# First norm with tokens on the partitions and transposes on TensorE, x loaded a second time; out projection, second norm and first FFN blocks interleaved by tile; last third of the FFN by tile

## What is computed

```python
mod = (jax.nn.silu(c) @ w_ada[l] + b_ada[l])[:, None, :]
sh1, sc1, ga1, sh2, sc2, ga2 = jnp.split(mod, N_MOD, axis=-1)
h = rms_norm(x, g_mix[l]) * (1 + sc1) + sh1
z = h @ w_in[l] + b_in[l]          # q k v | conv B, C, x | two gates; 50 blocks of 128 columns
attn = sliding_window_sink_attention(q, k, v, sinks[l])      # window 128, 16 heads of 64
conv = conv_b * causal_depthwise_conv(conv_c * conv_x, conv_w[l])
merged = jax.nn.sigmoid(gate_a) * attn + jax.nn.sigmoid(gate_c) * conv
x = x + ga1 * (merged @ w_out[l])
h = rms_norm(x, g_ffn[l]) * (1 + sc2) + sh2
gu = h @ w_ffn_in[l]
g_part, u_part = jnp.split(gu, 2, axis=-1)                   # 2816 each
x = x + ga2 * ((jax.nn.silu(g_part) * u_part) @ w_ffn_out[l])
return rms_norm(x, g_final)
```

## Time and profile before

| | us |
|---|---|
| three runs, median (lowest, highest) | 1123.89 (1123.4, 1236.33) |
| the profiled execution | 1121.86 |
| its span, core 5 | 1120.3 |
| spans of all cores | 1116.9 to 1120.3 |
| TensorE busy | 973.4 |
| VectorE busy | 634.0 |
| ScalarE busy | 350.8 |
| GpSimd busy | 250.6 |

### The profile page before, as it was taken

How to read it: one execution, slowest core, us unless ns; L and a number is a source line. 1 busy time by engine, 2 the same in 40 slices (tenths; PEclk the granted TensorE clock), 3 DMA queues, 4 the chain that set the end, 5 groups by cost and what they waited for, 6 DMA issues and landing times.

```text
span 1120.3 us, 15109 instructions; the slowest of 8 cores (1116.9 to 1120.3 us)
## 1 busy us (share of the span) xinstructions
PE 973.4 (87%) x5445; PEld 446.8 (40%) x5445; DVE 634.0 (57%) x834; ACT 350.8 (31%) x525; POOL 250.6 (22%) x276
## 2 busy tenths in 40 slices
PE   0273629999999999999979999999999999999972
PEld 0141214444444444444434434444444444444441
DVE  3449575595877969696977651134222243112697
ACT  3144124555454545454334321100111100111331
POOL 3405342121202111121365610000100001000460
PEclk9997669999999999999999999999999999999985
DMA  9950215886303031221610433210522205200124
GB/s 214 199 144 0 38 28 86 121 114 73 47 11 57 10 49 29 29 39 20 95 19 1 75 48 48 38 20 1 85 38 38 38 1 73 40 10 1 51 101 150
DMA packets 42201, 63.84 MB, mean 57 GB/s; under 512 B 19200, under 2 KB 21376, under 8 KB 40080
## 3 DMA queue, kind: packets, MB, share of 16 engines
q0 software_dynamic: 20304, 45.36, 26.6%
q1 hardware_dynamic: 21824, 17.52, 5.4%
HBM read 99.76 MB, written 8.45 MB: 97 GB/s over the span
## 4 chain that ended last, share of the span: by engine, by line
PE 79%; DVE 8%; issue 6%; ACT 3%; DMA 3%; POOL 1%; SPq 0%; DVEq 0%; ACTq 0%; POOLq 0%
PE psum L524 32%; PE psum L880 25%; PE psum L893 12%; PE psum L836 4%; PE psum L677 3%; DVE h L467 3%; DMA xres<-xt 3%; DVE xres L911 2%; PE psum L653 2%; POOL sqB L479 1%; DVE rs L455 1%; ACT L453 1%; PE psum L450 1%; DVE h L460 0%; DVE rden L702 0%
## 5 line engine op out<-in xcount | busy, mean ns | idle before, releaser
L524 PE MATMUL psum<-h,ws 128*128 128x512 bf16 (+2 forms) x1744 | 374.3, 368 | 23.1 <-DVE h L467 23.1
L880 PE MATMUL psum<-h,fws 128*128 128x512 bf16 x1408 | 305.7, 379 | 6.3 <-DVE h L467 4.9
L524 PEld LDWEIGHTS psum<-h,ws 128*128 128x128 bf16 x1744 | 163.0, 99 | 201.8 <-issue 51.0
L880 PEld LDWEIGHTS psum<-h,fws 128*128 128x128 bf16 x1408 | 137.3, 98 | 174.2 <-issue 9.7
L888 DVE TENSOR_TENSOR mg<-psum,sg 128x512 bf16<-128x512 f32 x88 | 60.6, 691 | 221.2 <-PE psum L880 216.4
L893 PE MATMUL psum<-mg,fwo 128*128 128x512 bf16 (+1 forms) x760 | 157.3, 370 | 11.5 <-DVE xres L900 9.9
L885 ACT ACTIVATE sg<-psum 128x512 bf16<-128x512 f32 x88 | 52.5, 597 | 336.3 <-PE psum L880 331.1
L702 DVE RECIPROCAL rden<-rden 128x256 f32<-128x256 f32 x64 | 110.5, 1737 | 7.7 <-ACT rden L700 7.2
L893 PEld LDWEIGHTS psum<-mg,fwo 128*128 128x128 bf16 x760 | 75.5, 100 | 94.4 <-issue 15.5
L900 DVE SCALAR_TENSOR_TENSOR xres<-psum,modc,xres 128x512 f32<-128x512 f32 (+1 forms) x104 | 72.0, 704 | 66.1 <-PE psum L893 66.1
L828 POOL TENSOR_TENSOR acc<-acc,sq 128x512 f32<-128x512 f32 (+1 forms) x56 | 79.6, 1426 | 116.1 <-ACT sq L826 111.8
(11 more groups left out here) (95 smaller groups left out, 716.1 us busy)
## 6 DMA issues: line engine op xcount, KB each, us to landing
ws<-w_in_l POOLq DMA_DIRECT2D x50, 256.0 KB, 4.7
fws<-w_fi_l POOLq DMA_DIRECT2D x44, 256.0 KB, 4.8
xres<-xt SPq DMA_DIRECT2D x8, 1024.0 KB, 18.4
wadaB<-w_ada_l POOLq DMA_DIRECT2D x8, 1024.0 KB, 10.1
out<-xres SPq DMA_DIRECT2D x12, 512.0 KB, 3.2
fwo<-w_fo_l POOLq DMA_DIRECT2D x22, 256.0 KB, 6.4
wadaA<-w_ada_l POOLq DMA_DIRECT2D x4, 512.0 KB, 24.0
wadaB<-w_ada_l POOLq DMA_DIRECT2D x4, 512.0 KB, 37.1
```

Source lines behind the costliest of these rows:

```text
L524: P.op("pe", [lambda e, k=k: e.matmul(bank(b)[:, 0:n], lhsT=WS[s * 1024 + k * 128, s * 1024 + (k + 1) * 128], rhs=hk(k, col, n), start=(k ...
L880: P.op("pe", [lambda e, k=k, s=s, b=b: e.matmul(bank(b), lhsT=FS[s * 1024 + k * 128, s * 1024 + (k + 1) * 128], rhs=hk(k, 128 + tt * 512, ...
```

## The change

First norm. x is loaded with tokens on the partitions (`xtok`, new input, same bytes). `stats` squares 1024 channels of 128 tokens at a time on ScalarE with the sum as a by-product, `roots` takes root and reciprocal of one value per token, `scale` multiplies by that (into `xn`, bf16), and `turn` transposes the 8 x 4 blocks of a tile on TensorE, 8 to a PSUM bank, and reads them out of PSUM with scale and shift applied, into `h`. The sums on GpSimd and VectorE, the fp32 matmuls, the reciprocal of 512 columns, `scaled` and `affine` are gone for the first norm. `prep` of tile t + 1 stands ahead of tile t's projections and `turned` behind them. The halo's k and v are made behind tile 0's projections.

Loads. x tile 1 waits for the second quarter of `wadaB`, the weights of slots 4 to 7 and the mask for x tile 1, x tile 2 for tile 1 and tile 3 for tile 2. In step c = 3 all of x is loaded again, in the old layout, 8 MB.

Second norm. `scaled` becomes 8 instructions of 512 columns at a later priority. Out projection, second norm and the first three FFN blocks are written in the order w0 w1 w2 f0 w3 f1 f2 f3, and all 8 banks are in rotation from w0 on. In the last third of the FFN, whose 14 weight blocks are now all loaded ahead, each tile runs `ff_in`, `ff_out` and the final norm before the next tile starts.

The planner. For every engine but TensorE it now takes, of the ready operations that could start within 0.25 us of the first, the one of lowest priority number. Operations of the same role are at L522 (`turn`), L556 (`mods_cols`), L584 (`group`), L607 (v transposes), L712 and L736 (attention), L900 (`w_out`), L468 (fp32 matmul), L953 (`ff_in`) and L966 (`ff_out`) of the new file.

```diff
--- before.py
+++ after.py
...
+    WINDOW = 0.25
...
-            best = None
+            first = None
             for e in self.ENGS:
                 f = free[e]
                 for o in ready[e]:
-                    k = (max(f, o.start), o.prio, o.idx)
+                    k = max(f, o.start)
+                    if first is None or k < first[0]:
+                        first = (k, e)
+            e = first[1]
+            lim = first[0] + (0.0 if e == "pe" else self.WINDOW)
+            best = None
+            for o in ready[e]:
+                at = max(free[e], o.start)
+                if at <= lim:
+                    k = (o.prio, o.idx)
                     if best is None or k < best[0]:
-                        best = (k, o)
+                        best = (k, o, at)
...
+    XN0 = buf("xn0", A_AT + 12320, 4096, BF16)
+    XNH = buf("xnH", A_AT + 20512, 1024, BF16)
+    XN = buf("xn", A_MG + 4096, 4096, BF16)
...
+    F2 = buf("fws2", A_K, 4096, BF16)
+    F3 = buf("fws3", A_AT + 34848, 2048, BF16)
...
-        P.op("sp", lambda e: e.dma_start(out=XH.t[:], in_=xhalo_d), writes=[XH.iv()], dma="d_xh", cost=0.1, nbytes=524288)
...
-        load_x(0)
-        load_x(1)
+        load_x(0, xtok_d)
+        P.op("sp", lambda e: e.dma_start(out=XH.t[:], in_=xhalo_d), writes=[XH.iv()], dma="d_xh", cost=0.1, nbytes=524288)
...
-        load_x(2, after=(last_wa,))
+        x1 = load_x(1, xtok_d, after=(wa_parts[1],))
         for zi in range(4, 8):
-            load_z(zi)
-        load_x(3, after=(last_wa,))
+            load_z(zi, after=(x1,))
...
+        x2 = load_x(2, xtok_d, after=(x1,))
+        load_x(3, xtok_d, after=(x2,))
...
+        def stats(src, a, nblk, s0, out):
+            for i in range(nblk):
+                P.op("act", lambda e, i=i: e.activation(out=out[i * 1024, (i + 1) * 1024], in_=src[a + i * 1024, a + (i + 1) * 1024],
+                                                        func=AF.Square, accum_out=SS[s0 + i, s0 + i + 1]),
...
+        def roots(s0, n):
+            P.op("act", lambda e: e.activation(out=RSTD[s0, s0 + n], in_=SS[s0, s0 + n], func=AF.Sqrt, bias=EPSC.t[:], scale=1.0 / D),
...
+            P.op("dve", lambda e: e.reciprocal(out=RSTD[s0, s0 + n], in_=RSTD[s0, s0 + n]),
...
+        def turn(xn, nblk, hcol, bks, engs):
...
+                P.op("pe", [lambda e, j=j, i=i, g=g, tp=tp: e.transpose(tp[:, j * n + i * 128:j * n + (i + 1) * 128],
+                                                                 xn[i * 1024 + (g * per + j) * 128, i * 1024 + (g * per + j + 1) * 128],
+                                                                 IDENT.t[:]) for j in range(per) for i in range(nblk)],
...
+                        P.op("dve", lambda e, k=k, src=src: e.tensor_scalar(out=hk(k, hcol, n), in0=src, scalar1=A1[k, k + 1],
+                                                                            scalar2=MODC[k, k + 1], op0=ALU.mult, op1=ALU.add),
...
+        def prep(tt):
+            stats(X, tt * 4096, 4, 1 + 4 * tt, XN)
+            roots(1 + 4 * tt, 4)
+            scale(X, tt * 4096, 4, 1 + 4 * tt, XN, ("act", "dve", "act", "dve"))
+
+        def turned(tt):
+            turn(XN, 4, 128 + 512 * tt, None, ("dve",))
...
+        turn(XN0, 4, 128, (4, 5, 6, 7), ("dve", "act"))
+        turn(XNH, 1, 0, None, ("act", "dve"))
...
+            load_wada(v, WA[1], 2, after=(marks[-1],))
...
+                if c == 3 and i < 4:
+                    load_x(i, xt_d, after=(marks[-1],))
...
+        def second_norm(tt):
...
+            P.prio = pos[0] + 9
+            for k in range(8):
+                a = tt * 4096 + k * 512
+                P.op("dve", lambda e, a=a, k=k: e.tensor_tensor(out=hk(k, 128 + 512 * tt, 512), in0=X[a, a + 512], in1=RS[ro + 512, ro + 1024], op=ALU.mult),
...
+        for what, tt in (("w", 0), ("w", 1), ("w", 2), ("f", 0), ("w", 3), ("f", 1), ("f", 2), ("f", 3)):
+            if what == "w":
+                for co in range(8):
+                    step_pos()
+                    w_out(tt, co)
+                second_norm(tt)
+            else:
+                for j in range(3):
+                    step_pos(2)
+                    ff_in(j, j, tt)
...
+                if last and lo == 0:
+                    for jl, j in enumerate(js):
+                        step_pos(2)
+                        ff_in(j, jl, tt)
...
                 if last:
+                    P.prio = pos[0] + (6 if i < len(tiles) - 2 else 3)
                     finish_tile(tt, lo, n, i)
```

168 lines of the change are left out of this document (96 added, 72 removed).

## The result

The changed kernel takes 0.962 of the time of the kernel before (95% interval 0.957 to 0.967). Its undisturbed runs are 1080.1 and 1082.6 us, those of the kernel before beside them 1123.4 to 1123.9. The forecast was 1043 us, with a range of 1029 to 1064, so the gain came out at about half and the time lies 16 us or more above the range.

The account below looks back on a forecast made before the run. TensorE was taken to bound the projections, leaving gains only at start, middle and end. Effective start 65, work 949, middle idling 7 and end 20.5 gave 1041.5 us, plus 1.6 outside the span: 1043 us, range 1029 to 1064.

Parts of the forecast that it names:

- The effective start: Start: when TensorE would have begun had it never waited; forecast to move from 120 to 65 us, 55 us gained.
- Transposes, 0.055 us each: Start: TensorE transposes run pipelined at 0.055 us each, 3.5 us for the 64 of tiles 2 and 3.
- One sign of being wrong: Start: a granted clock under 1.00 around the transposes would show the forecast wrong.
- Work without waits is 949 us: Whole kernel: TensorE's time without start, middle idling and end tail, 949 us, kept unchanged in the new sum.
- TensorE under 98% busy in c = 1 to 7: Projections: a sign of being wrong, which would be the planner's doing.
- The new rule costs nothing, VectorE has 26% of room: Projections: the planner's reordering of VectorE and ScalarE costs nothing, as VectorE has 26% of room.
- Middle, 8 us: Between attention and FFN: TensorE's idling falls from 14.9 to 7 us, 8 gained; bounds 3 and 14.9.
- behind 8 groups, 14 us: Middle: the norm's 12.9 us chain now stands behind 8 groups of TensorE work, 14 us, and not 5.
- the interleaving gives nothing: Middle, rival: the planner had already drawn FFN groups between out projections; 8 us back, 1051 us, chance 0.06.
- End, 15.5 us: Last third: the tail of final norms falls from 36 to 20.5 us, 15.5 gained.
- Second load of x, nothing: Projections, c = 3: loading x again, 8 MB, costs nothing with TensorE's 381 us as cover; without it 10 us.
- Slower: Projections, rival: the new planner rule makes VectorE wait in place and TensorE with it; 1125 us or more, chance 0.02.

Follow-up runs that it names:

- e1: Changed kernel with the four conditioning matmuls of c = 1 and 2 written eleven steps behind their 4 MB loads; 0.952, 1070 us.
- e2: Changed kernel with the 4 MB loads issued but the four late conditioning matmuls, their read-outs and transfers left out; 0.943, 1058.9 us.
- e4: Changed kernel with the 4 MB loads of the late conditioning vectors not held back by a mark; 0.960.
- e8: Changed kernel with conditioning matmuls late, w3 before f0, the old planner rule, two next-tile FFN blocks ahead of each tile's out blocks; 0.948, 1065 us.
- e12: e1 with the four VectorE sums behind the small transfers tied to the first query read-outs of c = 5; 0.949, 1068.6 us.
- e13: e8 with the four VectorE sums behind the small transfers moved to c = 5 and tied to its first query read-outs; 0.938, 1055.8 us.
- e3: Changed kernel with the planner's old rule (earliest start first, then priority); 0.958.
- e5: Changed kernel with the old middle: out-projection tiles one after another on four banks, norm product in one piece, then FFN blocks; 0.964.
- e7: Changed kernel with only the middle's order changed to w0 w1 w2 w3 f0 f1 f2 f3; 0.961.
- e6: Changed kernel with the old last third: block by block over four tiles, then their out blocks, final norms without lower priority; 0.976.
- e11: e8 with the four VectorE sums written in c = 5 and no second load of x; 0.9458, against 0.9462 with that load.

## Why the prediction was right and wrong

- **The effective start, 55 us gained: right.** 56.8 us at the end of c = 0 (56.9 in the mean of the cores). The order of events was the forecast one, to 1 us for the first projection and 4 us for `h` of tile 1. Some of it is borrowed: at that mark 20 fewer attention matmuls were done than before, about 1 us.
- **Transposes, 0.055 us each: right in kind.** All 96 filled 7.3 us, 0.076 each, where the sum had 5.3. The mean of one is 235 ns from start to end, and about three run within that time. One sign of being wrong came: the granted clock was 0.66 from 65 to 70 us, where 24 of them stand behind a wait of 2.2 us. It was 1.00 from 70 us on, with the other 72 among the projections. Whether the wait or the transposes lowered it, no run here separates. The Trainium skill ("TensorE: Matmul & The Clock Gate", part 4) has about 275 ns for one in a kernel, an estimated 26 us for 96; the trace agrees with that as a length and not as a price.
- **"Work without waits is 949 us", taken over unchanged: wrong, the largest miss, 23.4 us.** The sum treated c = 1 to 7 as the saturated stretch of before, 380.7 busy of 381. The step left an edit out: the list of the change never priced the new `after=(marks[-1],)` on a 4 MB load whose matmul stands right behind it. That load needs 17 us, and the matmul was due at once. e1, e2 and e4 show it. When the matmul was moved (e1, e8), a second wait came up that no row of before showed: VectorE waiting in order for a 16 KB transfer (e12, e13). In the kernel before the first three transfers were slow too, 11 to 17 us beside a load, but VectorE had 10 or more instructions to do between their issue and the sum (4 on core 6 of e8), and it waited at most 2.1 us for any of them. With both taken away c = 1 to 3 take 157.0 us in e13, 2.9 more than before. The prediction's own sign for this, TensorE under 98% busy in c = 1 to 7, came true (159.7 of 176.3 us in c = 1 to 3), but it put it down to the planner's rule, and e3 shows that the rule has little of it.
- **"The new rule costs nothing, VectorE has 26% of room": wrong by 4 to 5 us net.** Room on average does not help where TensorE waits for one instruction. In the mean of the cores the rule costs 2.6 us in c = 1 to 3, 1.0 in c = 4 to 7 and 2.2 in the middle, and gives 2.6 at the start (e3).
- **Middle, 8 us: wrong, it lost 3.2 on the slowest core and 0.4 in the mean.** The step that failed put the norm's 12.9 us "behind 8 groups, 14 us". It counted the length of one tile's chain and not VectorE's load: 20.00 of 20 us busy from 560 to 580. Where VectorE is full, moving the norm away from TensorE's wait moves it in front of a residual that TensorE waits for next. The interleaving gives 4 us in its stage (e5), the place of f0 takes 4 (e7) and the rule 2 (e3), and four of the eight cores wait 1.4 to 2.1 us for `w_out` weights, which none did before. The rival "the interleaving gives nothing", at a chance of 0.06, had the size right by luck: its reason, that the planner had already drawn FFN groups between, is not what e5 shows.
- **End, 15.5 us: the mechanism right, the size right against the same kernel (e6: 15.5), 11.6 against before.** Of the 3.9 us missed, 1.2 lie behind TensorE's last `ff_out` (18.2 for 17). TensorE's own waits are 5.2 us, 3.3 where each tile's `ff_out` waits for its last product, priced at 1.6 for the last tile alone, and 1.9 marked as issue. Two blocks of the next tile ahead of each `ff_out` went together with 1.4 us less in e8 than in e3, which has the same rule. The sum also took 6 us for the last half on TensorE where the earlier trace rows have 7.0 for 56 matmuls; the changed kernel took about 6.4 (28 in 3.22 us).
- **Second load of x, nothing: right** in time (e11), though it slowed a small transfer beside it.
- **The range.** The rivals were about the start, the loads and the middle. Only "Slower" (0.02) touched the projections: it had VectorE waiting in place and TensorE with it, which is the kind of wait that e8 shows, but from another cause, and it asked for 80 us of it. No rival had the load and its matmul. By step, 23.4 lost in c = 1 to 7, 11.2 missed in the middle and 3.9 at the end, less 1.8 more than forecast at the start, make the 36.7 us between 78.5 forecast and 41.8 measured.

## What to carry to other kernels

When a change takes idle time away at the start, what was done in that idle time must find another place: list each load that was issued there, when its data are due, and what is written behind its first reader. A matmul that waits holds more than itself: its PSUM banks, and by them the projections that come next in rotation. An instruction whose input comes by a slow small transfer belongs far behind it by a dependency, not by a priority, above all on an engine that everyone needs. And a stage is to be read on all cores: here one core's middle differs from another's by nearly as much as the change was to gain.

## What was not expected of the hardware

- A 16 KB transfer of single elements took 3.9 to 5.2 us without a large load beside it and 11.6 to 14.2 with one (changed kernel), and over 22 us on one core of e8 (issued at 195.03, VectorE released at 217.81), while on another core of the same run it let VectorE go at 199.18. One slow core sets the time of eight.
- The 4 MB load, 2 transfers of 1 MB written each, took 17 us while the projection weights went on; 16 MB of such loads left TensorE 152.6 of 154.1 us busy (e2).
- Two cores with nearly the same waits in the middle differ by 5.4 us; 4.6 of these are TensorE busy longer over the same matmuls, at a mean granted clock of 0.96 against 0.98 (e12).
